# First expert stage of a three-block transformer step: 64-slot passes in two column strips against 32-slot passes in four

## The reference

```python
logits = (h @ w_router) + b_router
top_v, top_i = lax.top_k(logits, 4)
gates = jax.nn.softmax(top_v, axis=-1)
# each expert e, on the tokens that chose it:
u = xb @ w_mlp1[e] + b_mlp1[e]               # 1024 -> 2048
x_glu = jnp.minimum(u[..., ::2], 7.0)
x_lin = jnp.clip(u[..., 1::2], -7.0, 7.0)
a = x_glu * jax.nn.sigmoid(1.702 * x_glu) * (x_lin + 1)
y = a @ w_mlp2[e] + b_mlp2[e]                # 1024 -> 1024
out[token] += gate * y
```

## Times and profile before

| | us |
|---|---|
| median of 3 runs (lowest to highest) | 2804.03 (2801.33 to 2805.39) |
| the profiled execution, its span | 2805.73, 2804.1 |
| TensorE busy | 2324.6 (83%) |
| VectorE, ScalarE busy | 577.4, 397.0 |
| bytes moved by DMA | 681.86 MB, mean 243 GB/s |
| up products of the stage (L966), busy | 527.3 + 247.8 |
| granted clock over the execution | 0.903 |

### The profile page before, as it was taken

How to read it: one execution, slowest core, us unless ns; L and a number is a source line. 1 busy time by engine, 2 the same in 40 slices (tenths; PEclk the granted TensorE clock), 3 DMA queues, 4 the chain that set the end, 5 groups by cost and what they waited for, 6 DMA issues and landing times.

```text
span 2804.1 us, 31586 instructions
## 1 busy us (share of the span) xinstructions
PE 2324.6 (83%) x12610; PEld 1264.3 (45%) x12611; DVE 577.4 (21%) x1319; ACT 397.0 (14%) x862; POOL 98.9 (4%) x131
## 2 busy tenths in 40 slices
PE   4976598989898989899898987799979998765564
PEld 3855322223222322233235866489965546332232
DVE  1043451111111111112111075200031202120002
ACT  1142110111101011111111143100001113110001
POOL 4000000000000000000000000000000000000000
PEclk9985689999999999999999997899989999867788
DMA  9460569999999799997963474246524342289975
GB/s 289 114 241 0 192 249 369 387 373 387 373 387 382 255 385 383 376 386 279 381 229 127 150 275 147 90 150 158 151 98 135 120 129 96 67 286 324 350 259 195
DMA packets 363561, 681.86 MB, mean 243 GB/s; under 512 B 15922, under 2 KB 122675, under 8 KB 363232
## 3 DMA queue, kind: packets, MB, share of 16 engines
q1 hardware_dynamic: 325616, 535.79, 54.6%
q0 software_dynamic: 37856, 144.98, 14.3%
q10 hardware_dynamic: 16, 0.02, 0.0%
HBM read 679.70 MB, written 1.06 MB: 243 GB/s over the span
## 4 chain that ended last, share of the span: by engine, by line
PE 68%; DMA 15%; DVE 7%; SPq 6%; ACT 3%; issue 1%; DVEq 0%; ACTq 0%
PE ps L664 29%; PE ps L966 15%; DMA ring<-in_w_mlp 11%; PE ps L988 5%; DMA MOD<-in_w 3%; PE ps L1259 3%; SPq L513 2%; PE ps L970 2%; SPq L514 2%; SPq L455 2%; PE ps L729 2%; PE ps L938 2%; PE ps L997 2%; DMA ring<-in_w_ada 1%; PE ps L831 1%
## 5 line engine op out<-in xcount | busy, mean ns | idle before, releaser
L966 PE MATMUL ps<-ring,scr 128*64 128x512 f32 x1680 | 527.3, 636 | 96.7 <-DMA ring<-in_w_mlp 95.0
L966 PEld LDWEIGHTS ps<-ring,scr 128*64 128x64 f32 x1680 | 158.8, 146 | 413.9 <-issue 412.9
L664 PE MATMUL ps<-ring,HTY 128*128 128x512 f32 (+5 forms) x960 | 328.4, 503 | 3.7 <-ACT HTY L1340 3.7
L664 PE MATMUL ps<-HTY,ring 128*128 128x256 f32 (+2 forms) x1392 | 298.8, 385 | 2.4 <-ACT HTY L1340 2.4
L664 PEld LDWEIGHTS ps<-HTY,ring 128*128 128x128 f32 (+2 forms) x1392 | 247.9, 182 | 51.2 <-ACT HTY L1340 3.6
L966 PE MATMUL ps<-MOD,scr 128*64 128x512 f32 x560 | 247.8, 595 | 0.0
L988 PE MATMUL ps<-HTY,scr 128*64 128x512 f32 x560 | 246.1, 592 | 1.0 <-ACT scr L1506 1.0
L988 PE MATMUL ps<-scr 128*64 128x512 f32 x560 | 246.1, 592 | 0.0
L664 PEld LDWEIGHTS ps<-ring,HTY 128*128 128x128 f32 x960 | 175.5, 191 | 153.4 <-issue 137.3
L2113 DVE TENSOR_SCALAR scr<-ps 128x256 f32<-128x256 f32 x70 | 29.7, 425 | 864.9 <-PE ps L970 864.9
L1259 PE MATMUL ps<-ring,scr 128*32 128x512 f32 x432 | 78.8, 709 | 111.5 <-DMA MOD<-in_w 110.8
(11 more groups left out here) (416 smaller groups left out, 2152.8 us busy)
## 6 DMA issues: line engine op xcount, KB each, us to landing
ring<-in_w_mlp SPq DMA_DIRECT2D x96, 2048.0 KB
MOD<-in_w_mlp SPq DMA_DIRECT2D x32, 2048.0 KB
HTY<-in_w_mlp POOLq DMA_DIRECT2D x32, 2048.0 KB, 10.4
scr<-in_w_mlp POOLq DMA_DIRECT2D x32, 2048.0 KB, 16.6
ring<-in_w_ada SPq DMA_DIRECT2D x24, 2048.0 KB, 9.1
ring<-in_w SPq DMA_DIRECT2D x48, 1024.0 KB, 11.7
ring<-in_w_in SPq DMA_DIRECT2D x21, 2048.0 KB, 7.8
ring<-in_w_ff SPq DMA_DIRECT2D x16, 2048.0 KB, 9.0
```

Source lines behind the costliest of these rows:

```text
L664: mm = pe.matmul(o, lhs(k), rhs(k), start=begin and k == 0, stop=end and k == nk - 1)
L966: pe.matmul(ps[C1 * s:C1 * (s + 1), b, :], XG[:, k, :], m1_slabs[2 * b + s][:, k, :], start=k == 0, stop=False)
```

## The change

A pass now has 32 slots (C1 = 32), and four products stand side by side in four column strips. `up` is no longer halved: all 2048 columns go through in one bank, 512 to a strip. The slabs of w_mlp1 are row blocks (256 rows of 2048 columns, runs of 8 KB), those of w_mlp2 row blocks of 512 rows (runs of 4 KB). `down` splits both its columns and its rows over the strips; the scatter sums over the two row halves. SP may ask for slab j of the next expert as soon as the last pass has used slab j (`m1_slab_used`), for slab 3 and the bias row after the whole up product. POOL still asks for slabs 4 and 5 after the down product.

The order in a pass is now: up of n, scatter of n-1, gather and token turn of n+1, hidden turn, way back and down of n. The first ranking uses `dve.max` and `dve.match_replace` in place of `ranks`; the first gather no longer waits for the gates, and the sums are started behind the first up product (`start_sums`). Per-pass lists of slots and gates are gone: VectorE reads the expert's number and takes its columns (`pick`).

TensorE's loop over passes, before, from the first half of up to the down product of the pass ahead (ps are the banks, ring, MOD, HTY and scr hold slabs and operands).

The core of the diff:

```diff
 FLOOR = -1.0e20
-C1 = 64
+C1 = 32
...
             def expert_slab(e, j):
-                cols_ = slice(BANK * j, BANK * (j + 1))
-                sp.dma_start(b1row[32 * j:32 * j + 1, :], I["b_mlp1"][0][e:e + 1, cols_] if isinstance(e, int)
-                             else I["b_mlp1"][0][bass.ds(e, 1), cols_]).then_inc(m1_landed[j], 16)
-                sp.dma_start(m1_slabs[j], kpn(I["w_mlp1"][0][e][:, cols_])).then_inc(m1_landed[j], 16)
+                sp.dma_start(m1_slabs[j], kpn(I["w_mlp1"][0][e][2 * P * j:2 * P * (j + 1), :])).then_inc(m1_landed[j], 16)
+
+            def expert_row(e):
+                sp.dma_start(b1row[0:P:32, :], I["b_mlp1"][0][bass.ds(e, 1), :].rearrange("e (c n) -> (e c) n", c=STRIPS))\
+                    .then_inc(m1_row_landed, 16)

             sp.wait_ge(product_ready, end["out1"])
             for j in range(3):
                 expert_slab(0, j)
             sp.wait_ge(h2_ready, NT)
+            expert_row(0)
             expert_slab(0, 3)
             sp.wait_ge(m1["counted"], 1)
             with sp.Fori(1, E1) as e:
                 through = sp.value_load(work[0:1, bass.ds(e + (THROUGH - 1), 1)], min_val=1, max_val=PASSES)
-                for j in range(4):
-                    sp.wait_ge(m1_up[j // 2], through)
+                for j in range(3):
+                    sp.wait_ge(m1_slab_used[j], through)
                     expert_slab(e, j)
+                sp.wait_ge(m1["up"], through)
+                expert_row(e)
+                expert_slab(e, 3)
             n_passes = sp.value_load(work[0:1, 0:1], min_val=E1, max_val=PASSES)
-            sp.wait_ge(m1_up[1], n_passes)
+            sp.wait_ge(m1["up"], n_passes)
...
+            def expert_slab(e, j):
+                pool.dma_start(m1_slabs[j], kpn(I["w_mlp2"][0][e][BANK * (j - 4):BANK * (j - 3), :])).then_inc(m1_landed[j], 16)
+
+            pool.wait_ge(mix_ready, 1)
+            expert_slab(0, 5)
-
-            def expert_slab(e, j):
-                pool.dma_start(m1_slabs[j], kpn(I["w_mlp2"][0][e][:, BANK * (j - 4):BANK * (j - 3)])).then_inc(m1_landed[j], 16)
-
             pool.wait_ge(product_ready, end["route1"])
             expert_slab(0, 4)
-            pool.wait_ge(gates_ready, 1)
-            expert_slab(0, 5)
...
+            pe.wait_ge(m1["masked"], 1)
...
                 for a in range(NT):
-                    for half in range(2):
-                        mm = pe.matmul(ps[C1 * half:C1 * (half + 1), 3, :], PICK[:, a, :], H[:, a, BANK * half:BANK * (half + 1)],
+                    for t in range(STRIPS):
+                        mm = pe.matmul(ps[32 * t:32 * (t + 1), 2, 0:S], PICK[:, a, :], H[:, a, S * t:S * (t + 1)],
                                        start=a == 0, stop=a == NT - 1)
                 mm.then_inc(m1["gather"], 1)
...
-            def up(n, b, e):
-
-                for j in (2 * b, 2 * b + 1):
-                    pe.wait_ge(m1_landed[j], 32 * e + 32)
+            def up(n, e):
+
                 if not (isinstance(n, int) and n == 0):
-
-                    pe.wait_ge(*((m1["up_read"], 2 * n - 1) if b == 0 else (m1["turn_read"], 2 * n)))
-                for k in range(KT):
-                    for s in range(2):
-                        pe.matmul(ps[C1 * s:C1 * (s + 1), b, :], XG[:, k, :], m1_slabs[2 * b + s][:, k, :],
-                                  start=k == 0, stop=False)
-                for s in range(2):
-                    r = 32 * (2 * b + s)
-                    mm = pe.matmul(ps[C1 * s:C1 * (s + 1), b, :], ones[r:r + 1, 0:C1], b1row[r:r + 1, :], start=False, stop=True)
-                mm.then_inc(m1_up[b], 1)
-
-            def turn_hidden(n, b):
-
-                pe.wait_ge(m1["hidden"], 2 * n + b + 1)
+                    pe.wait_ge(m1["up_read"], n)
+                for j in range(4):
+                    if j == 3:
+                        pe.wait_ge(m1_row_landed, 16 * e + 16)
+                    pe.wait_ge(m1_landed[j], 16 * e + 16)
+                    for k in (2 * j, 2 * j + 1):
+                        for t in range(STRIPS):
+                            mm = pe.matmul(ps[32 * t:32 * (t + 1), 0, :], XG[:, k, :], m1_slabs[j][:, k % 2, BANK * t:BANK * (t + 1)],
+                                           start=k == 0, stop=False)
+                    if j < 3:
+                        mm.then_inc(m1_slab_used[j], 1)
+                for t in range(STRIPS):
+                    mm = pe.matmul(ps[32 * t:32 * (t + 1), 0, :], ones[32 * t:32 * t + 1, 0:C1], b1row[32 * t:32 * t + 1, :],
+                                   start=False, stop=True)
+                mm.then_inc(m1["up"], 1)
+
+            def turn_hidden(n):
+
+                pe.wait_ge(m1["hidden"], n + 1)
+                if not (isinstance(n, int) and n == 0):
+                    pe.wait_ge(m1["back_read"], n)
                 for c in range(2):
-                    mm = pe.transpose(ps[:, 2 - b, P * c:P * (c + 1)], aS[:, b, P * c:P * (c + 1)], ident[:, :])
+                    mm = pe.transpose(ps[:, 1, P * c:P * (c + 1)], aS[:, P * c:P * (c + 1)], ident[:, :])
                 mm.then_inc(m1["turn"], 1)

             def down(n, e):
-                pe.wait_ge(m1["turn_read"], 2 * n + 2)
-                pe.wait_ge(m1["back_read"], n + 1)
+                pe.wait_ge(m1["turn_read"], n + 1)
                 for j in (4, 5):
                     pe.wait_ge(m1_landed[j], 16 * e + 16)
-                for k in range(KT):
-                    b, s_, c = k // 4, k // 2 % 2, k % 2
-                    for s in range(2):
-                        mm = pe.matmul(ps[C1 * s:C1 * (s + 1), 2, :], aT[:, 2 * b + c, C1 * s_:C1 * (s_ + 1)],
-                                       m1_slabs[4 + s][:, k, :], start=k == 0, stop=k == KT - 1)
+                for kk in range(4):
+                    for half in range(2):
+                        for s in range(2):
+                            t, c = divmod(4 * s + kk, 2)
+                            r = 64 * half + 32 * s
+                            mm = pe.matmul(ps[r:r + 32, 3, :], aT[:, c, C1 * t:C1 * (t + 1)],
+                                           m1_slabs[4 + s][:, kk, BANK * half:BANK * (half + 1)], start=kk == 0, stop=kk == 3)
                 mm.then_inc(m1["down"], 1)

             def scatter(n, last=False):

                 pe.wait_ge(m1["down_read"], n + 1)
+                pe.wait_ge(m1["back_read"], n + 1)
                 for a in range(NT):
                     for half in range(2):
-                        mm = pe.matmul(sum_bank(a, half), GPT[C1 * half:C1 * (half + 1), P * a:P * (a + 1)],
-                                       YS[C1 * half:C1 * (half + 1), :], start=False, stop=last, skip_group_check=True)
+                        r = slice(64 * half, 64 * (half + 1))
+                        mm = pe.matmul(sum_bank(a, half), GPT[r, P * a:P * (a + 1)], YS[r, :], start=False, stop=last,
+                                       skip_group_check=True)
                 mm.then_inc(m1["sum" if last else "scatter"], 1)

             def expert_of(n):
                 return pe.value_load(work[0:1, bass.ds(n + OF_PASS, 1)], min_val=0, max_val=E1 - 1)

-            def expert_pass(n, e, e_before):
+            def expert_pass(n, e):

                 pe.wait_ge(m1["gather_read"], n + 1)
-                up(n, 0, e)
-                if e_before is not None:
-                    turn_hidden(n - 1, 1)
-                    gather(n + 1)
-                    down(n - 1, e_before)
-                    turn_tokens(n + 1)
-                    up(n, 1, e)
-                    scatter(n - 1)
-                else:
-                    up(n, 1, e)
-                    gather(n + 1)
-                    turn_tokens(n + 1)
-                turn_hidden(n, 0)
+                up(n, e)
+                scatter(n - 1)
+                gather(n + 1)
+                turn_tokens(n + 1)
+                turn_hidden(n)
                 back(n)
+                down(n, e)

             pe.sem_inc(m1["scatter"], 1)
             pe.wait_ge(product_free, end["rank1"])
             gather(0)
             turn_tokens(0)
-            expert_pass(0, 0, None)
+            pe.wait_ge(m1["gather_read"], 1)
+            up(0, 0)
+            start_sums()
+            gather(1)
+            turn_tokens(1)
+            turn_hidden(0)
+            back(0)
+            down(0, 0)
             pe.wait_ge(m1["listed"], 1)
             n_passes = pe.value_load(work[0:1, 0:1], min_val=E1, max_val=PASSES)
             with pe.Fori(1, n_passes) as n:
-                expert_pass(n, expert_of(n), expert_of(n - 1))
-            turn_hidden(n_passes - 1, 1)
-            down(n_passes - 1, expert_of(n_passes - 1))
+                expert_pass(n, expert_of(n))
             scatter(n_passes - 1, last=True)

...
+            step(dve.memset(LOGITS1[:, :, 0:4], 1.0e30))
             dve.wait_ge(product_free, end["route1"])
```

(42 more changed lines are left out.)

230 lines of the change are left out of this document (97 added, 133 removed).

## The result

The changed kernel takes **2890.3 us** (median of 4 runs, 2885.1 to 2894.7) against 2802.7 us (2797.5 to 2805.4, 4 runs) before: the ratio is **1.0315, 95% interval 1.0295 to 1.0335**. It is slower by 88 us; the forecast was +76, and the mechanism that it named is the one that the trace shows. Two terms of its sum were wrong and nearly cancelled each other.

A forecast was written before the change was run, and what follows sets the result against it. Before, loads bound one-pass experts and TensorE the extra passes; after, late down slabs bind. 361 + 31 x 36.3 plus extra passes and 2.7 end the stage at 1561.7 against 1485.3: 2804.0 + 76 = 2880 us, range 2822 to 2924.

The forecast's parts named there:

- The share of the queues: Expert weight loads: packets alternate one for one, so POOL's 4 KB against SP's 8 KB gets a third, 0.139 MB/us.
- One-pass experts: First expert stage: an expert of one pass waits for POOL's down slabs and takes 36.3 us, against 32.5 before.
- POOL is alone for 1.7 us: Down-slab load: POOL moves 0.7 MB before SP's bytes start, then 3.5 MB at 0.139 take 25.2 us.
- The down product at the low clock: After TensorE idles 17 us the clock stays low, so the down product takes 6.0 us.
- The extra passes: Experts of two or three passes: +1.3 us per two-pass pair (five), 18.3 per three-pass (two), 11.3 and 14.9 for special cases.
- the run 23 to 26: Experts 23 to 26 wait for up slabs, two at 41.3 us: in all 11.3 us over four one-pass experts.
- The start: New routing ahead of the stage: first up product at 338.3, 21.5 us earlier; first down product ends at 361.
- The start of the sums: Behind the first up product: 8 instructions of 0.45 us, turn and copy, 4.8 us.
- A: Rival: loads never starve, both kinds of slab land together, stage ends 29 us earlier: 2775 us; chance 0.14.
- B: Rival: equal shares, SP's long runs travel as 4 KB, extra passes stop the DMA: +32, 2836 us; chance 0.16.
- C: Rival: long runs bring nothing, 387 GB/s in all, one-pass experts 38.0 us: 2934 us; chance 0.08.
- D: Rival: clock stays high through the waits, 2.5 us less at some 22 down products: 2825 us; chance 0.12.

The follow-up runs named there:

- The kernels with one pass for each expert: Changed kernel, and its one-queue variant, with every expert's passes set to one (tokens behind the 32nd left out): 2753.1 us with two queues, 2623.5 us with one.
- one queue: Changed kernel with the down slabs asked for by SP behind the same expert's up slabs, runs still 8 and 4 KB: 2780.2 us, ratio 0.991.
- 4 KB halves: Changed kernel with each up slab loaded by two DMAs of 1024 columns, so SP's runs are 4 KB: 2850.0 us, ratio 1.0149.
- with halves: Changed kernel with the down product behind the next pass's up and each up slab loaded by two DMAs of 1024 columns: 2854.8 us, ratio 1.0173.

## Why the prediction was right, and where it was not

**The share of the queues** (the forecast's main term): right. 0.140 MB/us against 0.139, one packet for one; 110 us of the kernel's time go when the sharing goes, and the kernel comes out faster than before instead of slower.

**One-pass experts, 36.3 us**: 34.1 to 34.6 measured, 2.1 too many, 65 us over the stage. The step that was off is "POOL is alone for 1.7 us". SP's first bytes came some 4 us after its issue, not 2.1: issue at 620.39, q0 alone through 622:624, and in 624:626 q1 sent 54 packets to q0's 106. POOL's head start is 3.7 us, in which it moves 1.1 of its 4.19 MB, and the rest takes 21.5 us, not 25.2; the down product can start 28.8 us behind the last one's end, not 30.3. The down product at the low clock: 5.5 to 5.9 against 6.0.

**The extra passes**, with 3.4 for expert 1: 72.7 us forecast, about 143 measured. Ends of down products in the trace after: an expert of two passes 36.9 to 37.1 (forecast 34.1), the one behind it 41.2 to 41.8 (39.7). Against two one-pass experts at 34.2 the pair costs 10, not 1.3. Of the 8.7 between, 4.2 are the base of two one-pass experts put too high. Of the other 4.5, 1.8 us is the first down product: it took 5.3 us, since TensorE had waited 2 us ahead of it and the clock fell again (a granted 0.77 over 452:459.5), where the forecast had it at full speed. A further 1.3 us is the landing of its slabs (15.0 us behind the last down product's end, forecast 13.7), and the rest is in the wait of the expert behind. Expert 29 and the one behind it cost only 7. Three passes with the next expert cost 26.7 and 26.1 over two one-pass experts (18.3), the run 23 to 26 20.8 (11.3), the last expert 19.7 (14.9). Sum by the measured terms: 366.0 + 31 x 34.2 + 4 x 10 + 7 + 20.8 + 2 x 26.7 + 19.7 + 2.5 = 1569.6, and the last down product did end at 1569.9.

**The start**: the first up product at 335.20 (forecast 338.3), the first down product's end at 366.0 (361). The start of the sums took 10.1 us instead of 4.8: TensorE waited 2.6 us for ScalarE, and the eight instructions ran from 348.70 to 355.89, 0.9 us each and not 0.45, at the low clock (granted 0.50 over 350 to 356); the first down product took 5.4 us, also mostly at the low clock (0.68 over 361 to 366). Routing alone brought 17.7 us to the kernel before.

**The sum**: 5 (start) - 65 (one-pass term) + 71 (extra passes) = +11, the difference of the stage's end (1572.64 against 1561.7). That the total came within 10 us is luck in so far as two terms of 65 and 71 cancel. The kernels with one pass for each expert show both.

**The rivals.** A, that the loads never starve, is what happens with one queue (2780.2 measured, 2775 by its sum): its terms for extra passes, 90 + 34 + 34 = 158 us, were right for a wire without sharing, where they measured 157. B, equal shares, was put at 2836, and 4 KB halves gave 2850. C, that long runs bring nothing: the wire moved 418 to 422 GB/s in this stage with 8 and 4 KB, against 387 in the earlier trace rows; it falls. The 387 is not SP's queue alone, as the prediction has it, but both queues: 4111 packets of 2 KB on SP's and 1126 of 4 KB on POOL's. The Trainium skill, "DMA: Bandwidth & Descriptors", section Specifications, has line rate at transfers of 512 bytes and up; the traces disagree, with 347 GB/s at 1 KB and 407 at 4 KB on SP's queue alone. D: the clock was 0.50 through the wait at 640 and the down product took 5.5 us; it falls.

**What has no price in the forecast**: the order of the down product. The forecast names it as the reason why late down slabs are waited for, but has no sum for the changed kernel without it. Moving it back alone gives 67 us (2890 to 2823). What is left open is how the loss of 110 us by sharing and that of 67 by order overlap: with the order early and one queue the kernel is at 2780, with the order late and two queues at 2823, and with both edits at 3057, so they are no two terms of one sum.

## What to carry to other kernels

Where two DMA queues are active at once, look at the bytes of their packets: here each queue got its share by packet, so the queue with the longer packets took most of the wire. Give them equal packets, or put both on one queue in the order in which the data are needed, and then let no wait stand in that queue ahead of loads that could go. And cutting TensorE's work by 226 us brought nothing where the loads set the pace: ask first how many microseconds in it no byte moves, and which wait holds them.

## What the runs showed of the hardware

- Packets of two busy queues went one for one whatever their size: 360 of 8 KB to 358 of 4 KB, as 127 to 124 in the earlier trace rows with 2 and 4 KB.
- SP's first bytes came about 4 us after its issue where POOL had been given two slabs just before (issues at 551.78, 620.39 and 1087.79 of the changed kernel), and 2.1 us or less (0.9 to 1.5 us, issue at 459.55 of the changed kernel) with POOL silent. POOL's came about 4 us after its issue behind a busy SP as well (issue at 544.48 with the down product late). Where the other queue was near the end of its slabs it was 1.2 to 2.5 us (SP's issues at 533.45 with the down product late, 1199.32 with halves).
- Four column strips start a new four every 0.43 us at the high clock, as two strips start a new pair, and every 0.83 us or so at the low one (here 7.0 us for the 16 fours of an up product).
- Loads of 1 MB with 4 KB runs out of rows of 8 KB began at 210 to 300 GB/s for some 4 us and went on at 407 or more; loads of 2 MB with such runs had no such start. The cause wasn't tried.
